# Recurrence levels one to three and four to six computed in one visit each, from copied operands

## What is computed

```
u = rmsnorm(h) @ w_in                   # q, f, i, g: 1024 columns each
q = silu(q); k = (1 - lb) * sigmoid(-f); log_f = log_sigmoid(f) + log1p(lb * exp(-f)); v = i
S_t = diag(f_t) S_{t-1} + k_t v_t^T     # per head
o_t = S_t^T q_t
y = (rmsnorm(o) * silu(g)) @ w_out;  h = h + y
```

## Time and profile before

| what | us |
|---|---|
| median of three runs | 985.9 |
| span of the profiled execution | 984.2 |
| TensorE matmul busy | 962.7 |
| VectorE busy | 577.2 |
| GpSimd busy | 406.1 |
| ScalarE busy | 380.9 |

### The profile page before, as it was taken

One profiled execution on the slowest core, in us unless ns is written; L12 is line 12 of the kernel. 1 busy time (PEld: TensorE's weight loads), 2 busy tenths in 40 slices (PEclk: granted clock), 3 DMA queues, 4 the chain that ended last, 5 costly groups with the idle time before them and its releaser, 6 DMA issues.

```text
span 984.2 us, 23595 instructions
## 1 busy us (share of the span) xinstructions
PE 962.7 (98%) x9958; PEld 902.2 (92%) x9958; DVE 577.2 (59%) x1195; ACT 380.9 (39%) x766; POOL 406.1 (41%) x295
## 2 busy tenths in 40 slices
PE   6999999999999999999999999999999999999996
PEld 6989999999999999899999999999998888788896
DVE  6455555555464645656942234456667857977635
ACT  7521322231313133424432223442127767866423
POOL 2265455454536363512225541441104534445343
PEclk9999999999999999999999999999999989999999
DMA  9521222223131312332324422321112222332104
GB/s 362 181 66 54 82 69 66 78 58 92 43 111 26 110 45 91 111 110 66 135 80 151 156 88 82 117 66 59 49 43 82 71 65 78 120 101 73 47 30 144
DMA packets 52921, 89.96 MB, mean 91 GB/s; under 512 B 15720, under 2 KB 34760, under 8 KB 52688
## 3 DMA queue, kind: packets, MB, share of 16 engines
q1 hardware_dynamic: 52528, 88.10, 27.9%
q10 hardware_dynamic: 288, 0.35, 0.1%
HBM read 70.80 MB, written 17.64 MB: 90 GB/s over the span
## 4 chain that ended last, share of the span: by engine, by line
PE 92%; DMA 3%; DVE 1%; SPq 1%; ACT 1%; issue 1%; POOL 0%; DVEq 0%; ACTq 0%
PE G L1657 64%; PE G L1954 9%; PE R L1716 3%; PE R L1885 2%; PE R L1899 2%; DMA ST<-xs 2%; PE R L1738 1%; PE R L1727 1%; PE R L1919 1%; PE R L1741 1%; PE R L1929 1%; PE R L1657 1%; PE R L1688 1%; PE R L1747 1%; DMA FG<-head_scales 1%
## 5 line engine op out<-in xcount | busy, mean ns | idle before, releaser
L1657 PE MATMUL G<-XH,WH 128*128 128x344 f32 x1160 | 377.4, 328 | 7.9 <-ACT XH L915 7.9
L1657 PE MATMUL G<-XL,WH 128*128 128x344 f32 x1160 | 370.3, 322 | 1.5 <-DVE XL L1285 0.8
L1657 PE MATMUL G<-XH,WL 128*128 128x344 f32 x744 | 235.6, 320 | 0.0
L1657 PEld LDWEIGHTS G<-XH,WH 128*128 128x128 f32 x1160 | 218.3, 189 | 16.2 <-issue 12.8
L1657 PEld LDWEIGHTS G<-XL,WH 128*128 128x128 f32 x1160 | 218.1, 189 | 4.6 <-issue 3.2
L682 POOL TENSOR_TENSOR WL<-WR,WH 128x1024 fp32r<-128x1024 f32 x40 | 103.3, 2582 | 159.8 <-ACT WH L826 159.8
L1657 PEld LDWEIGHTS G<-XH,WL 128*128 128x128 f32 x744 | 139.7, 188 | 0.0
L1657 PE MATMUL G<-XL,WL 128*128 128x344 f32 x416 | 133.3, 320 | 0.0
L826 ACT ACTIVATE WH<-WR 128x1024 fp32r<-128x1024 f32 x58 | 61.2, 1056 | 182.8 <-PE G L1657 156.7
L713 POOL TENSOR_TENSOR K<-K,FP 128x512 f32<-128x512 f32 x48 | 76.7, 1597 | 91.1 <-PE R L1716 91.1
L759 POOL TENSOR_TENSOR SP<-SP,small 128x1024 f32<-128x1024 f32 (+1 forms) x32 | 57.2, 1787 | 115.1 <-DVE small L1506 115.1
(11 more groups left out here) (272 smaller groups left out, 1719.2 us busy)
## 6 DMA issues: line engine op xcount, KB each, us to landing
WR<-w SPq DMA_DIRECT2D x58, 512.0 KB, 3.8
A<-x SPq DMA_DIRECT2D x8, 516.0 KB, 7.3
FG<-head_scales SPq DMA_DIRECT2D x8, 516.0 KB, 3.6
RESO<-x SPq DMA_DIRECT2D x8, 516.0 KB, 4.7
h_spill<-H SPq DMA_DIRECT2D x8, 516.0 KB, 2.9
gate_spill<-EV SPq DMA_DIRECT2D x24, 172.0 KB, 2.0
RES<-h_spill SPq DMA_DIRECT2D x24, 172.0 KB, 2.8
SS<-states SPq DMA_DIRECT2D x8, 512.0 KB, 5.4
```

Of the source, the lines that this page charges most:

```text
L1657: return nc.tensor.matmul(U[unit_bank(NU * n + i)][:, 0:TU], w[:, n % 3, k, :], x[:, seg(i)], start=(k == 0 and p == 0), stop=(k == KT - 1 ...
```

## The change

Levels 1, 2 and 3 are computed in one visit in slot 2, and levels 4, 5 and 6 in one in slot 5. To let the updates of levels 1, 2, 4 and 5 go ahead before TensorE has read them, the operands are copied first: VectorE copies the upper queries (`copy_queries`) to the head's row of A, which is unused until its output arrives; ScalarE copies the lower keys (`copy_keys`) to KTT (levels 1 and 4) or VK (levels 2 and 5). Values and keys are both turned in slot 6. The updates, merges and copies are moved to the slots given in the diff, on GpSimd and ScalarE in slot 3 ahead of the weight cuts. Two pairs of semaphores are merged into one each (`sums_done`, `ln_done`), which moves nothing. The same matmuls are done as before.

```diff
+LEVEL_VISITS = {2: (1, 2, 3), 5: (4, 5, 6)}
+COPIED = {1: 0, 2: 1, 4: 2, 5: 3}
 def turn_groups(it):
...
-        for s in range(1, NL):
-            slots[s].append((f"L{s}", rec, "dve"))
-        slots[2] += [("VT0", rec, "act"), ("VT1", rec, "act")]
-        slots[7] += [("T0", rec, "act"), ("T1", rec, "act")]
+        for at, levels in LEVEL_VISITS.items():
+            slots[at] += [(f"L{l}", rec, "dve") for l in levels]
+        slots[6] += [("VT0", rec, "act"), ("VT1", rec, "act"), ("T0", rec, "act"), ("T1", rec, "act")]
...
+    def level_queries(r, l):
+        return A[:, r, half(COPIED[l] % 2)]
+    def level_keys(l):
+        return (KTT, VK)[COPIED[l] % 2]
```

On GpSimd:

```diff
         def update_k(r, l):
-            pool.wait_ge(group_done, group_value(r, f"L{l}" if l else "D3"))
+            if l in COPIED:
+                pool.wait_ge(k_copied, copied(r, l))
+            else:
+                pool.wait_ge(group_done, group_value(r, f"L{l}" if l else "D3"))
...
             for slot in range(9):
+                if slot == 3 and r >= 0:
+                    for l in (3, 4, 5):
+                        update_k(r, l)
                 if slot % 3 == 0:
                     prepare(3 * it + slot // 3 + 2)
...
                 if slot == 0:
                     products(r)
-                if slot < NL:
-                    update_k(r, slot)
-                if slot == 4:
+                    for l in (0, 1, 2):
+                        update_k(r, l)
+                if slot == 5:
+                    update_k(r, 6)
                     decode_parts(r)
```

On ScalarE:

```diff
+        def copy_keys(r, l):
+            act.wait_ge(upd_k, NL * r + l)
+            if r and l == 1:
+                act.wait_ge(group_done, group_value(r - 1, "S1"))
+            if r and l == 2:
+                act.wait_ge(ss_done, r)
+            nc.scalar.activation(by_blocks(level_keys(l)[:, 0:SEQ], l)[:, :, 0, :],
+                                 by_blocks(K[r % 2][:, 0:SEQ], l)[:, :, 0, :], ACT.Copy).then_inc(k_copied, 1)
...
             for slot in range(9):
+                if slot == 3 and r >= 0:
+                    copy_keys(r, 4)
+                    copy_keys(r, 5)
                 if slot % 3 == 0 and (it or slot):
                     prepare(3 * it + slot // 3 + 2)
...
-                if slot == 3 and r >= 0:
-                    copy_turned(r, "VT", VH[:].rearrange("p c w -> p (c w)"))
+                if slot == 1 and r >= 0:
+                    copy_keys(r, 1)
+                    copy_keys(r, 2)
...
-                if slot == 8 and r >= 0:
+                if slot == 7 and r >= 0:
+                    copy_turned(r, "VT", VH[:].rearrange("p c w -> p (c w)"))
                     copy_turned(r, "T", KTT[:, 0:SEQ])
```

On VectorE:

```diff
+        def copy_queries(r, l):
+            dve.wait_ge(upd_q, NL * r + l)
+            nc.vector.tensor_copy(level_queries(r, l).rearrange("p (n h) -> p n h", h=1 << l),
+                                  by_blocks(QU[:], l)[:, :, 1, :]).then_inc(q_copied, 1)
...
                     if slot == 0:
                         first_query(r)
+                        update_q(r, 1)
+                        update_q(r, 2)
                         for c in range(NC // 2):
                             merge_diagonal(r, c)
-                    if 0 < slot < NL:
-                        update_q(r, slot)
-                        merge_level(r, slot)
+                    if slot == 2:
+                        for l in (3, 4, 5):
+                            update_q(r, l)
+                    if slot == 5:
+                        update_q(r, 6)
+                    for l in LEVEL_VISITS.get(slot, ()):
+                        merge_level(r, l)
```

On TensorE:

```diff
         def level(r, l):
-            pe.wait_ge(upd_q, NL * r + l)
-            pe.wait_ge(upd_k, NL * r + l)
+            if l in COPIED:
+                keys = level_keys(l)
+                pe.wait_ge(q_copied, copied(r, l))
+                pe.wait_ge(k_copied, copied(r, l))
...
-                    if 0 < slot < NL:
-                        level(r, slot)
-                    if slot == 2:
+                    for l in LEVEL_VISITS.get(slot, ()):
+                        level(r, l)
+                    if slot == 6:
                         pe.wait_ge(unit_read, 9 * r + 9)
                         transposed(r, "VT", RAWV)
-                    if slot == 7:
                         pe.wait_ge(upd_k, NL * r + NL)
                         transposed(r, "T", K[r % 2])
```

More of the change, by code:

```diff
@@ L288, in build @@
     upd_k = sem("upd_k")
+    q_copied = sem("q_copied")
+    k_copied = sem("k_copied")
     fp_step = sem("fp_step")
@@ L319, in build @@
     sq1_added = sem("sq1_added")
-    sums1_done = sem("sums1_done")
-    ln1_done = sem("ln1_done")
+    sums_done = sem("sums_done")
+    ln_done = sem("ln_done")
     rb1_done = sem("rb1_done")
@@ L372, in build @@
     sq2_added = sem("sq2_added")
-    sums2_done = sem("sums2_done")
-    ln2_done = sem("ln2_done")
     rb2_done = sem("rb2_done")
@@ L423, in decay, with copied @@
         return FP[:, at + odd:at + (SEQ >> l):2]
+    def copied(r, l):
+        return len(COPIED) * r + COPIED[l] + 1
+    def level_queries(r, l):
+        return A[:, r, half(COPIED[l] % 2)]
+    def level_keys(l):
+        return (KTT, VK)[COPIED[l] % 2]
     def by_blocks(ap, l):
@@ L998, in rms @@
         def rms(turn):
-            act.wait_ge(sums1_done, turn)
+            act.wait_ge(sums_done, turn)
             for i in range(NU):
                 ins = nc.scalar.activation(RB[:, seg(i)], R[i][:, 0:TU], ACT.Ln, scale=1.0 / D, bias=eps[:])
-            ins.then_inc(ln1_done, 1)
-            act.wait_ge(ln1_done, turn)
+            ins.then_inc(ln_done, 1)
+            act.wait_ge(ln_done, turn)
             nc.scalar.activation(RB[:], RB[:], ACT.Exp, scale=-0.5).then_inc(rb1_done, 1)
@@ L1109, in rms_segment @@
         def rms_segment(i):
-            act.wait_ge(sums2_done, i + 1)
-            nc.scalar.activation(RB[:, seg(i)], R[i][:, 0:TU], ACT.Ln, scale=1.0 / D, bias=eps[:]).then_inc(ln2_done, 1)
-            act.wait_ge(ln2_done, i + 1)
+            act.wait_ge(sums_done, i + 2)
+            nc.scalar.activation(RB[:, seg(i)], R[i][:, 0:TU], ACT.Ln, scale=1.0 / D, bias=eps[:]).then_inc(ln_done, 1)
+            act.wait_ge(ln_done, i + 2)
             act.wait_ge(gated, NQ)
@@ L1707, in level @@
             h = LEVELS[l]
-            pe.wait_ge(upd_q, NL * r + l)
-            pe.wait_ge(upd_k, NL * r + l)
+            keys = K[r % 2]
+            if l in COPIED:
+                keys = level_keys(l)
+                pe.wait_ge(q_copied, copied(r, l))
+                pe.wait_ge(k_copied, copied(r, l))
+            else:
+                pe.wait_ge(upd_q, NL * r + l)
+                pe.wait_ge(upd_k, NL * r + l)
             b = open_group(r, f"L{l}")
@@ L1715, in level @@
                     first = c * P + v * w
+                    if l in COPIED:
+                        queries = level_queries(r, l)[:, first // 2:(first + w) // 2].rearrange("p (n h) -> p n h", h=h)
+                    else:
+                        queries = by_blocks(QU[:, first:first + w], l)[:, :, 1, :]
                     ins = nc.tensor.matmul(b[v * w + shift:v * w + w - h + shift, first // 2:(first + w) // 2].rearrange(
                                                "p (n h) -> p n h", h=h),
-                                           K[r % 2][:, first:first + w - h],
-                                           by_blocks(QU[:, first:first + w], l)[:, :, 1, :], start=True, stop=True)
+                                           keys[:, first:first + w - h], queries, start=True, stop=True)
             ins.then_inc(group_done, 1)
```

9 lines of the change are left out of this document (6 added, 3 removed).

## The result

The changed kernel takes 998.59 us (median of 4 runs, 995.99 to 1000.3), the kernel before 986.07 (4 runs, 985.83 to 987.6): ratio 1.0125, 95% interval [1.011, 1.014]. The forecast was 988.4, its range ended at 991.5. The profiled span grew from 984.2 to 995.8, by 11.6 us.

The account below looks back on a forecast made before the run. TensorE was taken to bound the kernel, busy 962.7 of 984.2 us. Terms -5.6 + 1.9 + 2.25 + 5.25 - 1.3 = +2.5 gave 986.7, with 1.7 around the span 988.4 us; range 984.0 to 991.5.

Parts of the forecast that it names:

- the price of the matmuls in a merged visit: Small matmuls in merged visits: unchanged, 64 taking 0.65 us, with no extra cost for a neighbour inside a visit.
- B: Last iteration, slot 3: TensorE waits 2.25 us for the third square, behind key copies 4 and 5 and the weight cut.
- Rival 3: Small matmuls of levels 1 to 5 run slower in one long burst, 13 ns each: 6.9 us more, 995.2; chance 0.08.
- Visits: Heads 0 to 6: four visits fewer per head at 0.20 us each, 5.6 us gained; head 7 gains nothing.
- Cover in heads 0 to 6: Key updates and copies in heads 0 to 6 finish before TensorE wants them, 2.7 us to spare at level 3; cost 0.
- rival 2: Level 3 waits in every head because vector operations hold the key updates: 7.2 us on top, 995.5; chance 0.09.
- A: Last iteration, slot 1: TensorE waits 1.9 us for head 0's sum, whose square stands behind two key copies on ScalarE.
- C: Last iteration, slot 6: TensorE waits 5.25 us for level banks (3.95 turning values, 1.3 turning keys), freed by late merges.
- The 1.3 us that went: Last iteration: TensorE's existing 1.3 us of waits for query updates go, since these now lie two slots ahead.
- nothing comes back there: After slot 8 TensorE waits for no read in either case, so none of the last iteration's delay is recovered.
- a change of the tiling mode drains TensorE: Merged visit, level 5 followed by level 6: a drain would take 0.6 us of the gain; left out of the sum.
- The shared ports: Last iteration: vector copies could hold a key update in slots 1 and 3, at most 0.7 us each; sum 3.9, not 2.5.

Follow-up runs that it names:

- the kernel that has the changed order without a stop: The changed kernel with level 3 in its own visit in heads 0 to 6, and 23 tiny matmuls ahead of the first unit: 990.13 us, ratio 1.0049.

## Why the prediction was wrong

**The step that failed** is the price of the matmuls in a merged visit: "The small matmuls themselves are the same, 64 or fewer per level; I keep their price", and "a neighbour inside a visit costs nothing extra". For 64 next to 16 in the earlier trace rows that held. For 192 in one burst TensorE runs out of instructions. In the profiled run this costs 3.9 us in head 1 (stop and half clock), 2.1 in head 4 (stop alone), and in head 7 4.0 and by estimate 1.7, of which B gives back 1.4: 10.3 us together. Rival 3 had the right place, the long burst, and the wrong mechanism (some ns more for each matmul); it therefore gave 995.2 and 0.08.

The other steps, against the kernel that has the changed order without a stop (990.13, with one visit more in seven heads, 7 x 0.28 = 2.0; so 988.1 for the change itself):

- Visits: -5.6 forecast; 0.28 a visit instead of 0.20, so -7.8. The price was read from entry and exit alone; the levels beside each other also run closer (64 in 0.53 to 0.60 us, not 0.66).
- Cover in heads 0 to 6: right. No wait for keys or queries in heads 0 to 6 (rival 2 out), and the changed kernel's iterations without a block's edge late in the burst take 46.25 to 46.37 us.
- A 1.9 forecast, 1.5 measured; B 2.25 and 1.8. In the changed kernel B shrank to 0.4, because the unit ahead of it ran at half clock. C 5.25 and 4.2 + 1.1 = 5.3.
- The 1.3 us that went: right.
- Missing: the clock. Around C the stop-free kernel too has 10.2 us at half clock (415.4 to 425.6); by the changed kernel's row above, of the same length with 6.84 busy, that is by estimate 3.4 us. The forecast took a wait at its own length.

The sum of these terms is -7.8 + 1.5 + 1.8 + 5.3 - 1.3 + 3.4 = +2.9 us. The forecast's +2.5 is near it by luck: 2.2 us too little gain from the visits and 0.9 too much of A and B stand against 3.4 of clock that it didn't have. With the 10.3 of the stops the sum is 13.2, and the medians differ by 12.5. In the profiled execution the span grew by 11.6: it starts 0.4 us earlier, the seven iterations are 1.6 shorter (the terms say 1.8), the stretch from head 7's diagonal to its state sums is 14.4 longer (the terms say 15.0), and 0.8 come back behind it. The forecast was that nothing comes back there; the granted clock around 820 us is 0.50 for 3.4 us where it was 0.50 for 6.8 before. I can't place the 0.6 between 15.0 and 14.4.

The rule of the Trainium skill, TensorEngine Tiling (Array Packing), Key Properties, that a change of the tiling mode drains TensorE (0.6 us by the prediction) isn't to be seen: the version with only the upper levels together, the ones with 32 and 64 columns as neighbours, gains as much per visit as the others.

The shared ports showed in the vector copies and not in the key updates: the updates beside the first two in the last iteration took 1.54 and 1.37 us (at 384 and 386), no longer than the 1.60 of the earlier trace rows, and 30 of the 32 copies ended 0.27 to 0.29 us after a key update of GpSimd that had begun before them. They took 1.17 to 1.68 us, the one that began with GpSimd idle (57.95) 0.43. The Trainium skill, SBUF — State Buffer, the section on SBUF's two separate sides, states that whichever of the two begins first holds the pair for its whole instruction; the rows agree, and the prediction took only the case in which the copy is first.

Still open: why half clock follows some stops and not others (one of the six in the kernel with level 2 thrice), and what sets the moment at which a block's transfer begins.

## What to carry over

Before putting small matmuls together, count TensorE's instructions in the burst (here 32 small fp32 matmuls are 64 weight loads and 64 matmul records, and a wait is one more): in this kernel a burst of 258 cost nothing and one of 387 stopped in three of eight heads. Lengths between were not run. A stop whose place moves when unrelated instructions are put in front is the code stream, not a dependence. Price a long wait of TensorE with the half clock that can follow it, and when one wait of a chain is removed, look whether what is put ahead of others now waits itself.

## What the runs showed of the hardware

- TensorE's instructions come as 79 transfers of 16 KB. They took 0.93 to 1.45 us in the stops, and TensorE went on 1.2 to 1.5 us after the landing. In heads 0 to 6 the transfer before a stop began 0.7 to 1.1 us after the edge before it, in the last iteration, beside the norm's 516 KB read, 1.8 to 2.9.
- 387 records of small matmuls ran in 1.77 us, 4.6 ns each.
- A VectorE copy of 512 elements between SBUF tiles took 1.20 us when GpSimd had begun a key update before it, and ended 0.3 us after that update (0.43 us with GpSimd idle at its start). The product of as many took 0.69 when it began ahead of the update:

```profile
400.08 0.69 DVE L1266 TENSOR_TENSOR QU<-QU,FP 128x512 f32<-128x512 f32 x1 [5.50 <-PE R L1777]
400.12 1.60 POOL L729 TENSOR_TENSOR K<-K,FP 128x512 f32<-128x512 f32 x1 [10.37 <-PE R L1777]
400.81 1.20 DVE L1252 COPY A<-QU 128x512 f32<-128x512 f32 x1
```
